# A relative-bias table written to DRAM in 128 copies by GpSimd instead of once by ScalarE's queue

## The reference, cut to what matters

```python
rel = jnp.clip(q_pos[:, None] - k_pos[None, :], -REL_CLIP, REL_CLIP) + REL_CLIP   # REL_CLIP = 128
bias = rel_bias.astype(jnp.float32)[:, rel]            # rel_bias: 8 heads x 257
scores = jnp.where(valid[None, None, :, None, :], scores + bias[None, :, None], -1e30)
probs = jax.nn.softmax(scores, axis=-1).astype(v.dtype)
```

## Time and profile before

| | us |
|---|---|
| median of three executions | 872.73 |
| the profiled execution's own time | 874.51 |
| its span in the trace | 872.8 |
| TensorE busy with matmuls | 805.4 |
| VectorE busy | 495.5 |
| ScalarE busy | 449.1 |
| GpSimd busy | 217.8 |

### The profile page before, as it was taken

How to read it: one execution, slowest core, us unless ns; L and a number is a source line. 1 busy time by engine, 2 the same in 40 slices (tenths; PEclk the granted TensorE clock), 3 DMA queues, 4 the chain that set the end, 5 groups by cost and what they waited for, 6 DMA issues and landing times.

```text
span 872.8 us, 10612 instructions
## 1 busy us (share of the span) xinstructions
PE 805.4 (92%) x3635; PEld 635.2 (73%) x3635; DVE 495.5 (57%) x649; ACT 449.1 (51%) x580; POOL 217.8 (25%) x126
## 2 busy tenths in 40 slices
PE   4999999999989999999999967899999999999970
PEld 3887766675756888888888866688787787877750
DVE  6613657647482222204012434689888898988865
ACT  5244536364552232323222221687878887887842
POOL 5454323132231344444444234000000000000013
PEclk9999999999998999999999966999999999999985
DMA  9565451512021253333338364999999999975945
GB/s 308 176 235 176 144 190 51 190 53 73 25 77 45 74 168 122 97 99 96 100 96 286 122 241 193 334 393 397 400 392 402 393 400 398 395 306 204 368 145 198
DMA packets 126632, 186.76 MB, mean 214 GB/s; under 512 B 9148, under 2 KB 61956, under 8 KB 126596
## 3 DMA queue, kind: packets, MB, share of 16 engines
q1 hardware_dynamic: 119156, 167.82, 54.3%
q10 hardware_dynamic: 5136, 10.08, 3.1%
q0 software_dynamic: 2304, 8.39, 2.7%
HBM read 158.99 MB, written 27.28 MB: 213 GB/s over the span
## 4 chain that ended last, share of the span: by engine, by line
PE 83%; DVE 7%; ACT 4%; issue 3%; DMA 2%; POOL 1%; ACTq 1%; DVEq 0%; SPq 0%
PE ps L946 24%; PE ps L948 23%; PE ps L947 23%; PE ps L1029 2%; PE ps L1009 2%; PE ps L1170 2%; PE ps L1018 1%; DVE w_lo L349 1%; PE ps L1193 1%; PE ps L1118 1%; ACT w_hi L338 1%; DVE rgate L1393 1%; PE ps L1177 1%; DMA x<-in_x 1%; ACT xn L878 1%
## 5 line engine op out<-in xcount | busy, mean ns | idle before, releaser
L343 POOL TENSOR_TENSOR w_lo<-raw,w_hi 128x1024 fp32r<-128x1024 f32 x72 | 176.0, 2448 | 289.5 <-ACT w_hi L331 289.5
L331 ACT ACTIVATE w_hi<-raw 128x1024 fp32r<-128x1024 f32 x73 | 76.9, 1057 | 169.2 <-PE ps L948 159.7
L946 PE MATMUL ps<-xn_hi,w_hi 128*128 128x512 f32 x352 | 144.3, 410 | 0.0
L948 PE MATMUL ps<-xn_hi,w_lo 128*128 128x512 f32 x352 | 138.1, 392 | 0.0
L947 PE MATMUL ps<-xn_lo,w_hi 128*128 128x512 f32 x352 | 137.9, 392 | 0.0
L946 PE MATMUL ps<-w_hi,xT_hi 128*128 128x512 f32 x256 | 105.6, 413 | 9.6 <-issue 4.2
L948 PE MATMUL ps<-w_hi,xT_lo 128*128 128x512 f32 x256 | 102.6, 401 | 0.0
L947 PE MATMUL ps<-w_lo,xT_hi 128*128 128x512 f32 x256 | 102.5, 400 | 0.0
L946 PEld LDWEIGHTS ps<-xn_hi,w_hi 128*128 128x128 f32 x352 | 66.3, 188 | 26.9 <-issue 13.8
L613 POOL DMA_INDIRECT raw_mg<-slots,slot_idx x7 | 6.9, 984 | 306.2 <-ACTq L929 297.3
L948 PEld LDWEIGHTS ps<-xn_hi,w_lo 128*128 128x128 f32 x352 | 66.4, 189 | 14.5
(11 more groups left out here) (260 smaller groups left out, 1461.1 us busy)
## 6 DMA issues: line engine op xcount, KB each, us to landing
raw<-in_w_in SPq DMA_DIRECT2D x52, 512.0 KB, 3.8
raw_mg<-in_exp_w_down SPq DMA_DIRECT2D x36, 512.0 KB, 8.7
raw<-in_exp_w_gate SPq DMA_DIRECT2D x28, 512.0 KB, 9.7
raw_a<-in_exp_w_gate SPq DMA_DIRECT2D x27, 512.0 KB, 9.8
raw_c<-in_exp_w_up SPq DMA_DIRECT2D x27, 512.0 KB, 8.7
slots<-raw SPq DMA_DIRECT2D x24, 512.0 KB, 6.5
raw_mg<-in_exp_w_up SPq DMA_DIRECT2D x21, 512.0 KB, 9.2
raw<-in_exp_w_up SPq DMA_DIRECT2D x16, 512.0 KB, 9.0
```

The source lines that it names most:

```text
L331: nc.scalar.activation(w_hi[:, b % HI_SLOTS, :], raw_buf(b), ACT.Copy)\
L343: eng.tensor_tensor(w_lo[:, b % HI_SLOTS, :], raw_buf(b), w_hi[:, b % HI_SLOTS, :].bitcast(F32), ALU.subtract)\
L946: pe.matmul(dst, hi_l, hi_r, start=start, stop=False)
L948: return pe.matmul(dst, lo_l, hi_r, start=False, stop=stop)
```

## The change

The store to DRAM is issued by GpSimd, not by ScalarE's queue, and writes the table of each head 128 times (a source that repeats, 8 partitions x 128 copies x 384 entries, 1.57 MB). GpSimd waits for it to land, then issues the load of `bias` itself, from rows now 383 entries apart in DRAM. The table is built in reverse (a fill of 127 and a copy of 257 entries read backwards), so `bias` is read forwards. These two copies stand on VectorE behind the `x_lo` operations. The fill, the store and the load leave their old places on VectorE, ScalarE's queue and SyncE. On GpSimd all of it stands between the low part of block 2 and the memset that gives `zero_done`; the wait for `bias_in` moves from behind block 8 to behind block 4. On VectorE `x_lo` of tile t - 2 now follows the norm of tile t. `xrT` loses five columns and `to_line` goes.

```diff
-    toep = nc.dram_tensor("toep", [HEADS, 3 * P], F32, kind="Internal").ap()
+    toep = nc.dram_tensor("toep", [HEADS, P, 3 * P], F32, kind="Internal").ap()
...
-            xrT = sb(s1, "xrT", [P, CONV + 4 + TOK])
+            xrT = sb(s1, "xrT", [P, CONV - 1 + TOK])
...
-            sb(s1, "pad_b1", [P, AREA_B - (NT * AW + 4 * P + 4 * P + AW + 2 * NPAIR * P + CONV + 4 + 7 * TOK)])
+            sb(s1, "pad_b1", [P, AREA_B - (NT * AW + 4 * P + 4 * P + AW + 2 * NPAIR * P + CONV - 1 + 7 * TOK)])
...
-            sb(s2, "to_line", [P, 8])
... block.sync
-            sp.wait_ge(S["toep_out"], 16)
-            sp.dma_start(bias[:, :, :], bass.AP(toep.tensor, 1, [[1, P], [3 * P, HEADS], [1, 2 * P]]))\
-              .then_inc(S["bias_in"], 16)
... block.gpsimd, behind the low parts of blocks 0 to 2
+            pool.wait_ge(S["toep_rev"], 2)
+            pool.dma_start(toep, probs[0:HEADS, 0, 0:3 * P].unsqueeze(1).to_broadcast([HEADS, P, 3 * P])).then_inc(S["toep_out"], 16)
+            pool.wait_ge(S["toep_out"], 16)
+            pool.dma_start(bias[:, :, :], bass.AP(toep.tensor, P - 1, [[3 * P - 1, P], [3 * P * P, HEADS], [1, 2 * P]]))\
+                .then_inc(S["bias_in"], 16)
+
             pool.memset(gate_buf[:, 0:2, :], 0.0).then_inc(S["zero_done"], 1)
             for b in range(AHEAD, B_PAIR + AHEAD):
                 split_lo(pool, b)
-                if b == B_PAIR:
+                if b == AHEAD + 1:
                     pool.wait_ge(S["bias_in"], 16)
-                    pool.memset(bias[0:CHUNK, :, 0:CHUNK], NEG).then_inc(S["bias_done"], 1)
+                    pool.memset(bias[0:CHUNK, :, 3 * CHUNK:4 * CHUNK], NEG).then_inc(S["bias_done"], 1)
... block.scalar
-            act.dma_start(probs[0:HEADS, 0, 0:2 * CLIP + 1], a["rel_bias"][0]).then_inc(S["relb_in"], 16)
+            act.dma_start(probs[0:HEADS, 1, 0:2 * CLIP + 1], a["rel_bias"][0]).then_inc(S["relb_in"], 16)
...
-            act.wait_ge(S["toep_filled"], 1)
-            act.dma_start(toep, probs[0:HEADS, 0, 0:3 * P]).then_inc(S["toep_out"], 16)
...
-                        take(b - 1, xrT[:, CONV - 1:CONV - 1 + TOK], ACT.Copy)
+                        take(b - 1, xrT[:, CONV - 1:], ACT.Copy)
... block.vector
-            dve.wait_ge(S["relb_in"], 16)
-            dve.tensor_copy(probs[0:HEADS, 0, 2 * CLIP + 1:3 * P],
-                            probs[0:HEADS, 0, 2 * CLIP:2 * CLIP + 1].to_broadcast([HEADS, P - 1]))\
-               .then_inc(S["toep_filled"], 1)
... behind the norm of tile t
-            for t in range(NT):
+                if t >= 2:
+                    x_lo(t - 2)
+            for t in range(NT - 2, NT):
                 x_lo(t)
 
+            dve.wait_ge(S["relb_in"], 16)
+            dve.tensor_copy(probs[0:HEADS, 0, 0:P - 1],
+                            probs[0:HEADS, 1, 2 * CLIP:2 * CLIP + 1].to_broadcast([HEADS, P - 1]))\
+               .then_inc(S["toep_rev"], 1)
+            dve.tensor_copy(probs[0:HEADS, 0, P - 1:3 * P], probs[0:HEADS, 1, 2 * CLIP::-1])\
+               .then_inc(S["toep_rev"], 1)
... bias_and_max
-                                           bias[:, h, 2 * P - 1:2 * P], ALU.mult, ALU.add))
+                                           bias[:, h, 0:1], ALU.mult, ALU.add))
...
-                                              scalar=DH ** -0.5, in1=bias[:, h, near - 1::-1],
+                                              scalar=DH ** -0.5, in1=bias[:, h, 2 * P - near:],
```

More of the change, by code:

```diff
@@ L235, in build @@
             "ident_done consts_pool consts_dve zero_done zeros_stored "
-            "g1_in chan_in diag_in sgu_in relb_in toep_filled toep_out bias_in bias_done route_in g2_in "
+            "g1_in chan_in diag_in sgu_in relb_in toep_rev toep_out bias_in bias_done route_in g2_in "
             "sgu_raw sguT_ps sguT_done mask_done sv_sq sv_stat sv_rstd sv_done sp_exp sp_done halved "
```

## The result

| | us |
|---|---|
| changed kernel, median of 4 runs | 904.01 (902.82 to 906.14) |
| kernel before, median of 4 runs | 872.69 |
| ratio, 95% interval | 1.0366 (1.0330 to 1.0403) |
| profiled execution: its own time, its span | 902.05, 900.3 |
| TensorE, VectorE, ScalarE, GpSimd busy | 811.4, 488.2, 449.1, 220.1 |

What follows compares the result with a forecast made beforehand. TensorE, 83% of the chain that ended last, was taken to bound the kernel. Idle time of 27.4 us plus 1.7 for the clock gave + 29.1, 903.6 against the profiled 874.5, so 902 as median; range 873 to 914.

Steps and rivals of the forecast that it cites:

- The chain and the slack: TensorE takes up block 3 at about 36.7 us; GpSimd's low part is done 5.7 us before; later waits are covered.
- Nothing from the order on VectorE: `x_lo` 0 before norm 3: the norm still waits out GpSimd's low part, 0 us; upper end 2.4 us later.
- The two copies: Table copies on VectorE: 0.6 us for both, hidden for VectorE, but GpSimd waits for them until 22.2 us.
- The forward read at 0: Reading `bias` forwards instead of backwards in 32 operations on VectorE: 0 us, with 1 us either way.
- Descriptors: GpSimd writing 1024 rows per DMA, between 0.98 and 7.9 us: taken as 1 for the store, 3 for the load.
- The landing: Store out of eight partitions: 31.3 us for the bytes over two paths plus 3.3 fixed; two paths had chance 0.56.
- eight paths: Rival for the store: bytes take 7.8 us, landing 11.1, TensorE waits 3.9, median 878; chance 0.16.
- rule of 2 us plus the bytes at 436 GB/s: Rule giving the store 5.6 us, so nothing would happen; the hidden case, 873, had chance 0.15.
- The gap: TensorE idle once, 27.4 us before block 3, from 36.7 until GpSimd's low part is done at 64.1.
- The clock: After TensorE's idle time its clock is low and matmuls come 0.42 us apart: 1.7 us added.
- The addresses at 0: Tiles moved by 32 bytes, off multiples of 64: 0 us for TensorE's matmuls, upper end 10 us.
- The sum: Whole change: 27.4 us of TensorE idle and 1.7 for the clock, + 29.1 us in total, median 902.

Runs made afterwards that it cites:

- 2: Kernel before with only VectorE's order changed, low part of turned x of tile t - 2 behind the norm of tile t: 871.21 us, ratio 0.9997.
- 6: Changed kernel with the old addresses, table in 32 partitions, the store's eight source rows in partitions 0, 4, 8 to 28: 871.98 us, ratio 1.0021.
- 3: Changed kernel with the addresses of the kernel before (`xrT` of 520 columns, `to_line` kept): 895.51 us, ratio 1.0286.
- 1: Kernel before with the changed addresses alone (`xrT` of 515 columns, no `to_line`): 875.03 us, ratio 1.0053.
- 10: Kernel before with `xn_hi`, `xn_lo` and `br_*` moved up by 64 bytes through a larger pad in front: 873.07 us, ratio 1.0032.
- 11: Kernel before with a 32-byte gap between `xn_hi` and `xn_lo`, so only `xn_lo` lies off a multiple of 64: 873.21 us, ratio 1.0032.
- 9: Kernel before with only the mixer's tiles moved (`xrT` of 515 columns, `to_line` kept): 874.88 us, ratio 1.0060.
- 12: Changed kernel, its addresses kept, with the store's eight source rows in partitions 0, 4, 8 to 28: 877.41 us, ratio 1.0091.
- experiment 4: Changed kernel with old addresses, store issued on ScalarE's queue, its wait and the load on SyncE, GpSimd's `bias_in` wait later: 882.17 us, ratio 1.0121.
- 5: Kernel of experiment 4 with GpSimd's wait for `bias_in` moved behind the powers for the gating norm: 869.60 us, ratio 0.9994.

## Why the prediction was right

The forecast of 902 us and of one gap before block 3 came true, and so did the cause that it gave. Two of its terms did not. Point by point, by its own steps:

- *The chain and the slack.* Right. TensorE was ready for block 3 at 60.42 - 24.66 = 35.8 (predicted 36.7; it had started early), and no later wait was added to the gap.
- *Nothing from the order on VectorE.* Right, shown by 2. In the changed kernel `x_lo` 0 ran at 13.60 and norm 3, queued at 14.74, ended at 17.0 as before.
- *The two copies.* GpSimd had the table at 22.23, predicted 22.2, but partly by luck: the copies took 1.30 and 0.27 us, not 0.6 together, and `x_lo` 3 ended at 20.5, 1.0 earlier than I had it.
- *The forward read at 0.* Right. The operations that read `bias` forwards take 424 ns in the median, as they did backwards.
- *Descriptors.* 1.34 us for the store (taken at 1) and 0.98 for the load (taken at 3). 1024 rows cost about what 128 do in the earlier trace rows; the upper bound of 7.9 was far off.
- *The landing.* The times in the DMA view run from the start of the issue, so 1.0 + 31.3 + 3.3 = 35.6 us was predicted, and 33.6 measured; for eight paths 1.0 + 7.8 + 3.3 = 12.1, and 10.7 measured in 6. The two times lie 22.9 us apart, the bytes over two and over eight paths at 25.1 GB/s 23.5. So 6 shows that the places of the partitions decide it; that they reach two paths and eight is inferred from these rates. In the rows of the kernel before nothing decided between one, two and eight; that I took two was a guess by them, and it came out right. The Trainium skill's "SBUF — State Buffer", section "Door 1: The DMA port swizzle", puts partitions 0 to 7 on two ports, and 0, 4 to 28 on eight. The measurements agree with these numbers, not quite with its rate: it gives 28.9 us for the bytes, at the 49 GB/s of the trace 1.57 MB take 32.1. The Trainium skill's rule of 2 us plus the bytes at 436 GB/s ("DMA: Bandwidth & Descriptors", section "Anatomy of one DMA"), which would have hidden the store, does not hold for such a source: 5.6 us by it, 33.6 measured.
- *The gap.* Predicted 27.4 us, measured 24.7. It ended 3.7 us before the predicted 64.1: the load's issue was 2.0 shorter, and the store had landed 1.7 earlier. It also began 0.9 earlier.
- *The clock.* Mis-sized: 1.7 predicted, about 3.1 measured, as block 3 took 69.08 - 60.42 = 8.7 us instead of 5.6. The mean granted clock of the stretch 60 to 70 us is 0.68, between full speed (2.4 GHz) and half. In 3, behind nearly the same gap, block 3 took 68.63 - 60.93 = 7.7 us instead of 5.44, 2.3 lost. I had one pause to take the price from, one of 2.3 us; the price differs between executions.
- *The addresses at 0.* Wrong: 4.6 us by 1 alone, 7 us beside the rest of the change. The failed step was to take a load of weights from `gu` as a stand-in for matmuls over `xn`. The bound of 10 us held, but 10 contradicts the 64-byte pieces that it was made from. The prediction's own sign for it, longer stretches after 100 us, came: 168 us for 163.
- *The sum.* Wait and clock were to cost 29.1 us and cost 24.9 (by 3); the addresses were to cost nothing and cost 7. That gives the measured 31 to 32 and, with the 4.6 us of the addresses alone, 29.5. That my 29.1 came within 3 us of the result is luck: one term too large by 4 stood against one too small by 7. The trace agrees with 3: when block 3 was done, the copy to `w_hi` that it releases was 68.63 - 42.51 = 26.1 us late in 3, and 69.08 - 42.51 = 26.6 in the changed kernel.

What stays open: why moving `xn_*` slows its matmuls by 6.7 ns. Experiments 10 and 11 rule out that an operand off a multiple of 64 bytes pays by itself; that the distance between tiles read together plays a part would fit both, but was not tested. Open, too, is why the kernels with moved tiles, run without the slow store (1, 9 and 12), are granted more clock.

## What to carry to other kernels

For a DMA out of or into few partitions, count the paths that these reach, not the bytes alone: spreading eight rows four partitions apart made the same store three times as fast (34.0 and 10.7 us). A full wait on an engine costs what stands behind it in program order, so before moving one, list that for the new place as well (experiment 4 forgot it, 5 mended it). And let no address move as a by-product of another edit in a kernel that TensorE paces; time it alone.

## What the runs showed that I had not expected

- 24 matmuls take 5.44 or 5.60 us by the placement of their tiles alone, 32 or 64 bytes being enough.
- TensorE's first blocks ran at full clock in some traces (copy to `w_hi` behind block 1 at 30.0 to 30.7 us) and not in others (31.5 to 32.0), independently of the edits: up to 2 us of spread between single executions.
- A store that keeps about half the DMA share busy at 49 GB/s made a 512 KB weight load so late that ScalarE waited 12 us for it (experiments 4 and 5); in the changed kernel this was hidden behind the gap, as the load of block 7 was issued only after it.
